# Input projection on unnormed, channels-first x, with the row factor applied to its results

## The reference

```python
def rms_norm(x, g):
    y = xf * lax.rsqrt(jnp.mean(xf * xf, axis=-1, keepdims=True) + NORM_EPS)
    return (y * g.astype(jnp.float32)).astype(x.dtype)

h = rms_norm(x, pre_mix_g[l])
z = h @ w_in[l]
za, zb, zc = jnp.split(z, [NA_IN_COLS, NA_IN_COLS + RW_IN_COLS], axis=-1)
ya = neighbourhood_attention(qa, ka, va, na_rpb[l])
yb = rwkv7_mixer(zb, ...)      # begins with token_shift: z + mu_prev*(z_prev - z) + mu_next*(z_next - z)
yc = retention_mixer(qc, kc, vc, gc)
y = jnp.concatenate([ya, yb, yc], axis=-1) @ w_out[l]
x = x + rms_norm(y, post_mix_g[l])
h = rms_norm(x, pre_mlp_g[l])
u = jnp.square(jax.nn.relu(h @ w_up[l])) @ w_down[l]
x = x + rms_norm(u, post_mlp_g[l])
```

## Time and profile before

| | |
|---|---|
| median of 3 runs | 1326.92 us (1324.72 to 1327.81) |
| span of the profiled execution | 1324.1 us |
| TensorE busy | 1301.0 us, 98% |
| VectorE busy | 814.0 us, 61% |
| ScalarE busy | 648.3 us, 49% |
| GpSimd busy | 305.4 us, 23% |
| moved by DMA | 226.44 MB, mean 171 GB/s |

### The profile page before, as it was taken

One profiled execution on the slowest core, in us unless ns is written; L12 is line 12 of the kernel. 1 busy time (PEld: TensorE's weight loads), 2 busy tenths in 40 slices (PEclk: granted clock), 3 DMA queues, 4 the chain that ended last, 5 costly groups with the idle time before them and its releaser, 6 DMA issues.

```text
span 1324.1 us, 25483 instructions
## 1 busy us (share of the span) xinstructions
PE 1301.0 (98%) x10563; PEld 1143.0 (86%) x10563; DVE 814.0 (61%) x1134; ACT 648.3 (49%) x1004; POOL 305.4 (23%) x255
## 2 busy tenths in 40 slices
PE   8999999999999999999999999999999999999997
PEld 7999888888899898888888888888888888888886
DVE  5557778777776977547555555555555555555565
ACT  6465664566434457447444444444444444444453
POOL 0011333234205221000555555555530000000000
PEclk9999999999999999999999999999999999999999
DMA  8656433333357444773866666666666666666672
GB/s 254 195 170 178 119 106 98 97 92 88 109 124 198 118 128 151 275 235 98 236 190 187 187 190 189 190 190 190 191 188 194 192 192 196 194 194 193 193 232 99
DMA packets 286099, 226.44 MB, mean 171 GB/s; under 512 B 15200, under 2 KB 263264, under 8 KB 285344
## 3 DMA queue, kind: packets, MB, share of 16 engines
q1 hardware_dynamic: 285456, 223.51, 57.6%
q0 software_dynamic: 240, 1.18, 0.3%
q10 hardware_dynamic: 288, 0.13, 0.0%
HBM read 222.69 MB, written 2.10 MB: 170 GB/s over the span
## 4 chain that ended last, share of the span: by engine, by line
PE 67%; DVE 3%; ACT 2%; DMA 1%; issue 1%; DVEq 0%; ACTq 0%
PE psum L2193 31%; PE psum L1812 18%; PE psum L1823 9%; PE psum L1796 2%; PE psum L1802 2%; PE psum L1797 2%; DMA raw<-in_w_out 1%; DVE w_lo L808 1%; ACT w_hi L1366 1%; PE psum L2169 0%; PE psum L2250 0%; DVE arena L1268 0%; PE psum L2071 0%; PE psum L2161 0%; PE psum L1958 0%
## 5 line engine op out<-in xcount | busy, mean ns | idle before, releaser
L808 DVE TENSOR_TENSOR w_lo<-raw,w_hi 128x1024 fp32r<-128x1024 f32 x394 | 496.6, 1263 | 390.5 <-ACT w_hi L1366 388.6
L1366 ACT ACTIVATE w_hi<-raw 128x1024 fp32r<-128x1024 f32 x394 | 418.8, 1065 | 447.0 <-PE psum L2193 189.1
L2193 PE MATMUL psum<-w_hi,act_both 128*128 128x512 f32 x1216 | 328.0, 390 | 1.6 <-DVE arena L1192 0.9
L2193 PEld LDWEIGHTS psum<-w_hi,act_both 128*128 128x128 f32 x1216 | 227.8, 188 | 50.4 <-issue 1.8
L1812 PE MATMUL psum<-act_both,w_hi 128*128 128x512 f32 x1024 | 247.0, 391 | 0.0
L1796 PE MATMUL psum<-act_both,w_hi 128*128 128x256 f32 x912 | 239.7, 296 | 0.5 <-ACT w_hi L1366 0.4
L1797 PE MATMUL psum<-act_both,w_hi 128*128 128x256 f32 x912 | 227.2, 283 | 0.0
L1812 PEld LDWEIGHTS psum<-act_both,w_hi 128*128 128x128 f32 x1024 | 188.1, 188 | 36.3
L2193 PE MATMUL psum<-w_lo,act_both 128*128 128x512 f32 x608 | 187.5, 389 | 0.0
L1796 PEld LDWEIGHTS psum<-act_both,w_hi 128*128 128x128 f32 x912 | 173.6, 190 | 8.9 <-issue 1.5
L1797 PEld LDWEIGHTS psum<-act_both,w_hi 128*128 128x128 f32 x912 | 174.2, 191 | 0.1
(11 more groups left out here) (240 smaller groups left out, 1069.8 us busy)
## 6 DMA issues: line engine op xcount, KB each, us to landing
raw<-in_w_up SPq DMA_DIRECT2D x128, 512.0 KB, 4.1
raw<-in_w_down SPq DMA_DIRECT2D x128, 512.0 KB, 4.5
raw<-in_w_in SPq DMA_DIRECT2D x114, 512.0 KB, 4.2
raw<-in_w_out SPq DMA_DIRECT2D x32, 512.0 KB, 4.7
arena<-in_x SPq DMA_DIRECT2D x4, 512.0 KB, 6.2
arena<-in_na_rpb SPq DMA_DIRECT2D x16, 128.0 KB, 4.4
arena<-in_x SPq DMA_DIRECT2D x1, 2048.0 KB, 9.6
out_x<-arena SPq DMA_DIRECT2D x3, 512.0 KB, 2.7
```

Of the source, the lines that this page charges most:

```text
L808: dve.tensor_tensor(by_half(h, low(h)), by_pair(h, raw[:, place[h] % RAW]), by_half(h, high(h)).bitcast(F32), ALU.subtract).then_inc(s["lo ...
L1366: act.activation(by_half(h, high(h)), by_pair(h, raw[:, place[h] % RAW]), ACT.Copy).then_inc(s["hi_half"], 1)
L2193: last = pe.matmul(bank[4 * t + 2 * j + b], lhs[:, tokens], w[:, b * 512:(b + 1) * 512], start=start, stop=stop)
```

## The change

The input x also comes channels first, in four blocks of four depths (512 KB each), each ahead of the two weight halves that need it. The vectors come channels first too. TensorE turns nothing at the start. ScalarE and VectorE split x times the gain, without the row factor. The row factor (one number per token, on all partitions) is made beside the projection: ScalarE squares the blocks, VectorE adds them over depth in four reductions and their total in a fifth, a matmul with ones adds over the partitions ahead of gap 10, ScalarE takes the root, VectorE the reciprocal.

The first four tiles (groups 0 and 1) run by depth blocks: a slot takes 4 depths of 2 tiles, and each weight load is 4 depths by 256 columns. All recurrence tiles use matmuls of 512 columns into a bank each (0, 1, 6, 7). Their results pass ScalarE (copy of one half), VectorE (sum), GpSimd (times the row factor), ScalarE (two scaled copies) and VectorE (shift). For the attention tiles GpSimd multiplies the stored result, for the retention queries and keys the tables of cosines and sines take the factor, and the last six groups (values and gates) are drained by VectorE with the factor in place of ScalarE. The order of the first tiles and the constants' layout change, and the bonus sum of the recurrence is two matmuls of 64 output rows in place of one of 128. The token shift of groups 0 and 1 is now due at 97 depths.

```diff
-RW_ORDER = [WD, AD, R_(0), K_(0), V_(0), V_(1), R_(1), K_(1), R_(2), K_(2), V_(2), V_(3), R_(3), K_(3), R_(4), K_(4),
+RW_ORDER = [WD, AD, K_(0), K_(1), R_(0), V_(0), V_(1), R_(1), R_(2), K_(2), V_(2), V_(3), R_(3), K_(3), R_(4), K_(4),
...
-HI_LAG, LO_LAG, DRAIN_LAG, SHIFT_LAG = 2, 5, 2, 6
+HI_LAG, LO_LAG, DRAIN_LAG = 2, 5, 2
+SUM_LAG, SCALE_LAG, ZS_LAG, SHIFT_LAG = 3, 4, 9, 13
+BLOCK_KT, BLOCK_T = 4, 4
+BLOCK_H = BLOCK_T * KT // HALF_KT
+NORM_GAP = 10
+ZS_FROM, SHIFT_FROM = 8 * NORM_GAP + 9, 8 * NORM_GAP + 17
...
 # SyncE
+            for q in range(KT // BLOCK_KT):
+                block = slice(q * BLOCK_KT, (q + 1) * BLOCK_KT)
+                sp.dma_start(x_in[:, block], x_t_d[:, block]).then_inc(x_block_in[q], 16)
+                fetch(2 * q)
+                fetch(2 * q + 1)
+            for h in range(BLOCK_H, BLOCK_H + 2):
+                fetch(h)
+            sp.dma_start(cst[:], cst_d).then_inc(s["consts_in"], 16)
...
 # GpSimd, in its gaps
+                pool.tensor_tensor(z, z, row_scale.unsqueeze(1).broadcast_to([P, len(tiles), T]), ALU.mult).then_inc(
+                    s["z_scaled"], 1)
...
 # VectorE
+            def add_squares(q):
+                dve.wait_ge(s["x_squared"], q + 1)
+                dve.tensor_reduce(x_part[:, q], x_sq[:, q].rearrange("p (k t) -> p t k", t=T), AX_X, ALU.add).then_inc(
+                    s["x_parted"], 1)
+            def total_squares():
+                dve.tensor_reduce(x_total, x_part.rearrange("p q t -> p t q"), AX_X, ALU.add).then_inc(
+                    s["x_totalled"], 1)
+            def row_factor():
+                dve.reciprocal(row_scale, row_scale).then_inc(s["row_ready"], 1)
+            for q in range(KT // BLOCK_KT):
+                split_x(q)
+                lo(2 * q)
+                lo(2 * q + 1)
+                if q >= 2:
+                    add_squares(q - 2)
...
 # VectorE, gap()
-                while at["shift"] < RW_GROUPS and KT * (group_tiles(at["shift"])[-1] + 1) + SHIFT_LAG <= done:
+                while at["shift"] < RW_GROUPS and max(complete(at["shift"]) + SHIFT_LAG, SHIFT_FROM) <= done:
                     shift(at["shift"])
                     at["shift"] += 1
+                while at["sum"] < RW_GROUPS and complete(at["sum"]) + SUM_LAG <= done:
+                    sum_z(at["sum"])
+                    at["sum"] += 1
+                while at["nr"] < GROUPS and complete(at["nr"]) + DRAIN_LAG <= done:
+                    scaled_nr(at["nr"])
+                    at["nr"] += 1
                 while at["lo"] < OUT_H + 2 and HALF_KT * (at["lo"] - SPLIT + 1) + LO_LAG <= reached(at["gap"]):
                     lo(at["lo"])
                     at["lo"] += 1
+                if at["gap"] in (NORM_GAP - 2, NORM_GAP - 1):
+                    add_squares(at["gap"] - NORM_GAP + 4)
+                if at["gap"] == NORM_GAP - 1:
+                    total_squares()
+                if at["gap"] == NORM_GAP + 1:
+                    row_factor()
...
 # ScalarE, start and gap(); to_zs of groups 0 and 1 is due from ZS_FROM on
+            for q in range(KT // BLOCK_KT):
+                split_x(q)
+                hi(2 * q)
+                hi(2 * q + 1)
+                if q:
+                    squares(q - 1)
...
+                while at["copy"] < RW_GROUPS and complete(at["copy"]) + DRAIN_LAG <= done:
+                    copy_z(at["copy"])
+                    at["copy"] += 1
                 while at["hi"] < OUT_H + 2 and HALF_KT * (at["hi"] - SPLIT + 1) + HI_LAG <= reached(at["gap"]):
                     hi(at["hi"])
                     at["hi"] += 1
+                if at["gap"] == NORM_GAP - 2:
+                    squares(KT // BLOCK_KT - 1)
+                if at["gap"] == NORM_GAP:
+                    row_root()
...
 # TensorE
-            keep_busy(8)
-            pe.wait_ge(s["ident_in"], 16)
-            for k in range(6):
-                turn_block(k, 0)
...
+            for _ in range(10):
+                pe.matmul(bank[5][:, 0:T], zeros[:, 0:P], zeros[:, 0:T], start=True, stop=True)
...
+                for kt, n, at in blocks:
+                    if n == 0:
+                        pe.wait_ge(s["h_lo"], kt + 1)
+                    pe.matmul(bank[rw_bank(n)], w_hi[:, h % SPLIT, at:at + P],
+                              act_both[:, kt].rearrange("p a t -> p (a t)"), start=kt == 0, stop=False)
...
+                if g == NORM_GAP:
+                    row_sum()
...
-                    pe.matmul(bank[2][:, T:2 * T], ones, tmp, start=True, stop=True)
+                    for e in range(2):
+                        pe.matmul(bank[2][e * C:e * C + C, T:2 * T], ones[:, e:e + 1].broadcast_to([P, C]), tmp,
+                                  start=True, stop=True)
```

More of the change, by code:

```diff
@@ L141, in constants @@
     half = np.arange(P) // C
-    put("ones", (half[:, None] == half[None]).astype(np.float32))
+    put("ones", (half[:, None] == np.arange(2)[None]).astype(np.float32))
     theta = np.float32(1.0) / np.float32(10000.0) ** np.linspace(0.0, 1.0, P // 2, dtype=np.float32)
@@ L377, in layer @@
         raw_in = [sem(f"raw_in{r}") for r in range(RAW)]
-        x_half_in = [sem(f"x_half_in{i}") for i in range(2 * TT)]
+        x_block_in = [sem(f"x_block_in{i}") for i in range(KT // BLOCK_KT)]
         block = ctx.enter_context(nc.Block())
@@ L455, in drained, with scaled, rw_halves @@
             eng.wait_ge(s["bank_free"], RW_GROUPS + j // 2 + 1)
+        def scaled(eng):
+            eng.wait_ge(s["na_scaled"], NA_T // 2)
+        def rw_halves(g):
+            tiles = group_tiles(g)
+            b = rw_bank(tiles[0])
+            return psum[:, b:b + len(tiles)].rearrange("p n (a t) -> p n a t", a=2)
         def due(depth):
@@ L710, in products @@
                 steps[0]()
+                gap()
                 run(early[0])
@@ L732, in chunk @@
                 return decay_state if n in (1, 2) else nothing, nothing, nothing
-            stage_a(nothing, feed, tilde, products, level, chunk, STARTS)
+            stage_a(gap, feed, tilde, products, level, chunk, STARTS)
+            assert at["scale"] == RW_GROUPS and at["na"] == NA_T // 2
+            pool.wait_ge(s["table_in"], 16)
+            turns = table[:, LATE["cos"][0]:LATE["sin"][1]].rearrange("p (a t) -> p a t", a=2)
+            pool.tensor_tensor(turns, turns, row_scale.unsqueeze(1).broadcast_to([P, 2, T]), ALU.mult).then_inc(
+                s["table_scaled"], 1)
             pool.wait_ge(s["bias_in"], 16 * ROWS * ROWS)
-            pool.wait_ge(s["table_in"], 16)
             win = late_const("win").unsqueeze(1).broadcast_to([P, TT * ROWS, GRID_W])
@@ L1825, in up_low, with block_slot, row_sum @@
                 return last
+            def block_slot(h):
+                q, pair = h // 2, h % 2
+                blocks = [(q * BLOCK_KT + i, 2 * pair + j, (2 * i + j) * P) for i in range(BLOCK_KT) for j in range(2)]
+                pe.wait_ge(s["hi_half"], h + 1)
+                for kt, n, at in blocks:
[3 more added lines that the diff above has]
+                              act_both[:, kt].rearrange("p a t -> p (a t)"), start=kt == 0, stop=False)
+                pe.wait_ge(s["lo_half"], h + 1)
+                for kt, n, at in blocks:
+                    last = pe.matmul(bank[rw_bank(n)][:, 0:T], w_lo[:, h % SPLIT, at:at + P], act_hi[:, kt],
+                                     start=False, stop=kt == KT - 1)
+                last.then_inc(s["gemm_half"], 1)
+            def row_sum():
+                pe.wait_ge(s["ones_set"], 1)
+                pe.wait_ge(s["x_totalled"], 1)
+                pe.matmul(bank[5][:, 0:T], all_ones, x_total, start=True, stop=True).then_inc(s["x_summed"], 1)
             at_gap = [0]
@@ L1853, in kk_sum @@
                     for a in range(TT):
-                        last = pe.matmul(bank[2][:, 2 * a:2 * a + 2], kk_sq[:, a * P:(a + 1) * P], ones[:, 0::C],
+                        last = pe.matmul(bank[2][:, 2 * a:2 * a + 2], kk_sq[:, a * P:(a + 1) * P], ones,
                                          start=True, stop=True)
```

264 lines of the change are left out of this document (143 added, 121 removed).

## The result

The changed kernel takes 1336.7 us (median of four runs, 1334.7 to 1339.4) where the kernel before takes 1326.0 on the same chip. The ratio is 1.0081, with a 95% interval from 1.0064 to 1.0098. It is 10.7 us slower; the prediction had it 4.7 us faster, and 1336.7 lies outside its range.

What follows compares the result with a forecast made beforehand. TensorE's work plus the start was taken as the bound. The terms -3.8 (at slot 16), -2.6 (slots), +0.5 (bonus) and +1.2 (late groups) gave -4.7 us, so 1322.2 us, range 1316.8 to 1328.5.

Steps and rivals of the forecast that it cites:

- Part 1, the slots: Projection with 512-column tiles: a slot takes 2.78 us instead of 2.88, gaining 2.6 us over 26 slots behind slot 16.
- Part 2, the start: Start without transposes, row factor or scaling of x: slot 0 begins at 10.0 us, and the start wins 10 us.
- the 9.5 us bound: Start: the ten zero matmuls end at 9.5 us if their pace changes on the way, 10.4 at the slow pace.
- Part 3, the row factor: Row-factor chain from gap 8: waits pile up at slots 13 and 14; slot 16 begins at 60.8, gaining 3.8 us.
- rival (c): Row sum: three late reductions with 1 KB steps take X, not 1.22 us; at four times, 1333 us; chance 0.15.
- the break-even at 2.8 us: Row sum: the time X of one strided reduction at which the gain of 4.7 us is gone.
- Rival (a): Slot 14: the same pile-up, and TensorE's clock falls in it, +2.2 us, giving 1324.4 us; chance 0.17.
- "A later group's chain has cover: nothing": Recurrence groups after the pile-up: a chain of about 5.4 us has two gaps and two buffered slots of cover, costing nothing.
- "GpSimd's scalings in the turns: nothing, up to 1": Turns: GpSimd's six scalings lie in a GpSimd that idles for VectorE and ScalarE, costing nothing, up to 1 us.
- Part 4, the bonus: Recurrence bonus sum: two matmuls of 64 rows replace one of 128, 0.1 us for each of six pairs, 0.5 in all.
- Part 5, the late groups: Last six groups: 128x512 results move from ScalarE to VectorE, costing 1.2 us, between -0.5 and 4.1.

Runs made afterwards that it cites:

- the best version: Changed kernel with recurrence and attention scalings on VectorE, packed sums, the square two gaps later and queries first: 1320.6 us, ratio 0.9961 to the kernel before.

## Why the prediction was wrong

**Part 1, the slots: right in pitch.** Slots 11 and 12 are 2.79 us apart (42.26, 45.05). But the forecast counted the shorter slots in full, and taking them back in the best version cost 1.2 us of 3.1.

**Part 2, the start: too late by 1.4 us.** Slot 0 begins at 8.6, not 10.0; the twenty records of zero matmuls took 6.88 us, less than the 9.5 us bound allowed.

**Part 3, the row factor: the queue was right, two sizes were not.** ScalarE did stand for the shifts, slot 13 came 0.56 late (1.1 said) and slot 14 3.57 (4.1 said), with w_hi 14 ready 15.9 us after slot 10 began (16.3 said). The reciprocal took 1.75 us (1.7 said) and GpSimd's scaling of two groups 2.46 (2.8 said). Wrong were:
- The reductions, 2.0 us and not 1.22. That is rival (c) at X = 2.0; its own rule, 3(X - 1.22), gives 2.3 us, and undoing it gave 3.0. It cannot explain the sign: the prediction put the break-even at 2.8 us.
- The clock. Rival (a) said +2.2; slots 14 and 15 took 3.3 us more than two slots, and filling the wait gave 2.4 back. The forecast had it at nothing.

Slot 16 therefore begins at 64.0 instead of 60.8.

**"A later group's chain has cover: nothing": the step that failed.** The cover was counted for the chain's own result (the shifted group), and up to turn 0 TensorE never waits for that. It was not counted for what the scaling delays by standing in GpSimd's queue. The scaling waits there for VectorE's sum, the queries stand behind it, ScalarE stands for the queries, and w_hi behind ScalarE. Up to turn 0 the forecast gained 2.6 us from slot 16 on and the kernel lost 5.9. Swapping the order alone gave 3.4 us back, scaling on VectorE 7.0. The 7.0 hold a second thing that the forecast had at nothing: GpSimd's operation stretches VectorE's beside it (the rows stand in the last section). How the other 3.6 us divide between this, the slower scaling itself and the clock was not taken apart.

**"GpSimd's scalings in the turns: nothing, up to 1": also wrong.** Undoing them gave 3.8 us, and in the traces 2.7 without the clock's share. GpSimd's idle time was real. But its operation stretches VectorE's, and in the turns TensorE waits for VectorE. The busy share of an engine said nothing about either.

**Part 4, the bonus: the matmuls were right, the first turn is open.** From the first bonus matmul to the next line it is 0.58 us (154.15 to 154.73) against 0.53 before (147.64 to 148.17), 0.05 more where 0.1 was said. But the first turn costs 1.6 us more in the changed kernel (38.7 against 37.1 us from its first key product to that of turn 1) and as much or more in the versions without GpSimd's scalings. In that turn TensorE has a wait of 1.0 us ahead of L2044 that the kernel before has not, and one of 0.8 us ahead of L2099 where before had 0.4. The profile shows nothing that ended the first of them, and no run took that part alone.

**Part 5, the late groups: between.** From the end of turn 5 on the changed kernel loses 0.5 us, the others 0 to 2.8 (1.2 said). Without GpSimd's scaling the output projection waits 1.1 and 0.8 us for w_lo, in the best version not at all. What sets that stays open.

**The sum.** The four faults of the design (scaling in GpSimd's queue, scaling beside VectorE, strided sums, the square's place) are worth 7.0, 3.8, 3.0 and 3.2 us. The first three were each undone in the changed kernel, the square in the best version; in the changed kernel moving it alone gave 0.9, inside the noise, because a second cause stood behind it. The sum of 17.0 is near the 15.9 between the changed kernel and the best one, whose gain of 5.2 us over before is what the prediction had promised for the change (4.7). The clock's share is inside these numbers. Of the rivals, none was "slower through GpSimd's queue"; the one on the slow side named another mechanism.

## What to carry to other kernels

An engine that is 25% busy is not free: before an instruction is put into its queue, write down what is queued behind it, how long it will itself wait, and who waits for that. An operation on GpSimd with operands in SBUF is also priced at what it adds to VectorE's instructions beside it. And where TensorE has no slack, a long wait costs more than its length: behind the 3.57 us at slot 14 two slots took 3.3 us too long in one trace and 1.8 in another, while the waits of 1.36 and 1.68 us in the best version cost only themselves.

## What the runs showed of the hardware

- **TensorE's clock after a wait.** In the stretch from 38 to 130 us, waits of 0.4 to 1.7 us were never followed by a low clock. All six waits of 3.1 to 3.6 us were, in six traces. Those from 2.1 to 2.9 us went either way, with the same kernel text around them: 2.11 us at the row sum fell in three traces and not in four, 2.2 us near 108 to 110 us fell in three and not in two. In the turns, in a stretch of matmuls of 32 and 64 columns, the wait of 1.25 us was followed by a fall in three of six traces and the one of 1.23 us in one of six. The Trainium skill (TensorE: Matmul & The Clock Gate, "Why this matters for your kernels") warns of idle gaps between bursts, and the six long waits agree. The same wait decides differently from run to run. A fall cost 1.4 to 1.5 us in the turns (209.8, 211.3 and 212.7 us with none, one and two) and 1.8 or 3.3 us at slots 14 and 15. It fits the spread of the times, though no run shows that it makes it: the four runs of the changed kernel take 1334.7 to 1339.4 us at a mean granted clock of 0.992 to 0.996, the nine of the best version 1320.0 to 1321.7 us at 0.998 to 0.999.
- **A reduction that steps by 1 KB.** 128x1024 f32 to 128x256 takes 2.0 us against 1.22 for packed rows of the same count, a factor of 1.64. The two also differ in how many sums they write (256 against 4), and no run takes the step alone. The Trainium skill (SBUF — State Buffer, "Door 1: The DMA port swizzle") was cited in the prediction for the direction, and the trace agrees with that.
- **GpSimd beside VectorE.** Of GpSimd's scaling and VectorE's w_lo, the one that starts second is stretched. The scaling of 128x512 takes 1.18 us when it runs alone or starts first (44.16, 55.08), and 2.05 to 2.3 when it starts just behind a w_lo (102.69, 247.10). When GpSimd is first by 0.11 us, w_lo takes 2.15 us instead of 1.23:

```profile
55.08 1.18 POOL L726 TENSOR_TENSOR arena<-arena,row_scale 128x512 f32<-128x512 f32 x1 [8.46 <-DVE arena L910]
...
55.19 2.15 DVE L895 TENSOR_TENSOR w_lo<-raw,w_hi 128x1024 fp32r<-128x1024 f32 x1 [0.25 <-ACT w_hi L1490]
```

On VectorE the same multiplication takes 0.69 us.
